# Two root-mean-square norms of a two-block transformer kernel: who sums the last tiles of squares, and when the first weight units are split

## What is computed

```python
def rmsnorm(x, g):
    y = x * rsqrt(mean(x * x, axis=-1) + EPS)
    return y * g

def first_block(x, ...):
    for i in range(2):
        h = rmsnorm(x, ln1_g[i]) @ w_in[i]          # cq, ckv, then the heads' k, q, v
        ...three groups of attention...
        x = x + concat(o_fox, o_diff, o_mla) @ w_o[i]
        up = causal_dwconv(rmsnorm(x, ln2_g[i]) @ w_up[i], ...)
        x = x + (silu(g) * u) @ w_down[i]
    return rmsnorm(x, final_g)

def second_block(x, c, ctx, ...):                   # ctx has 256 tokens
    for layer in range(2):
        h_lat = rms_norm(x, norm_g[layer]) * (1 + scale) + shift
        h_ctx = the same for ctx
        ...layer 0: mLSTM mixer; layer 1: windowed attention...
        x = x + gate * y
```

## Time and profile before

| | |
|---|---|
| median of 3 runs | 2538.12 us |
| the profiled execution | 2534.49 us |
| its span | 2532.8 us |
| mean granted clock of TensorE over the span | 0.993 |

### The profile page before, as it was taken

How to read it: one execution, slowest core, us unless ns; L and a number is a source line. 1 busy time by engine, 2 the same in 40 slices (tenths; PEclk the granted TensorE clock), 3 DMA queues, 4 the chain that set the end, 5 groups by cost and what they waited for, 6 DMA issues and landing times.

```text
span 2532.8 us, 32353 instructions
## 1 busy us (share of the span) xinstructions
PE 2466.3 (97%) x12450; PEld 2009.7 (79%) x12450; DVE 1217.8 (48%) x2205; ACT 986.0 (39%) x1731; POOL 977.3 (39%) x512
## 2 busy tenths in 40 slices
PE   9999999999999999999999999999999999899998
PEld 6986788888789678888888777878787778887766
DVE  4366599530245648974026522631251352556663
ACT  5465444432255545444333223131222322455552
POOL 3232365765433235576653223222222224322231
PEclk9999999999999999999999999999999999999999
DMA  4211254323321124532331111112111111111000
GB/s 177 67 55 67 92 189 169 101 94 98 116 67 55 67 84 150 192 111 96 105 119 57 52 42 59 51 34 67 51 59 42 50 50 46 58 59 34 30 21 34
DMA packets 54584, 200.48 MB, mean 79 GB/s; under 512 B 6176, under 2 KB 6176, under 8 KB 53664
## 3 DMA queue, kind: packets, MB, share of 16 engines
q1 hardware_dynamic: 52272, 189.27, 21.9%
q10 hardware_dynamic: 2160, 9.15, 1.0%
HBM read 196.29 MB, written 2.10 MB: 78 GB/s over the span
## 4 chain that ended last, share of the span: by engine, by line
PE 78%; DVE 15%; ACT 3%; issue 2%; POOL 2%; DVEq 0%; ACTq 0%; POOLq 0%
PE ps L890 25%; PE ps L557 19%; PE ps L577 16%; PE ps L607 11%; DVE arena L1953 7%; PE ps L782 2%; DVE arena L2142 1%; DVE arena L2139 1%; DVE norm_sq L1917 1%; PE ps L1203 1%; PE ps L798 1%; POOL norm_acc L2606 1%; POOL wl L2593 1%; DVE hl L1929 1%; PE ps L1007 1%
## 5 line engine op out<-in xcount | busy, mean ns | idle before, releaser
L2593 POOL TENSOR_TENSOR wl<-wring,wh 128x1024 fp32r<-128x1024 f32 (+1 forms) x305 | 770.0, 2525 | 1246.5 <-ACT wh L1243 1234.7
L1243 ACT ACTIVATE wh<-wring 128x1024 fp32r<-128x1024 f32 (+1 forms) x305 | 317.1, 1043 | 544.4 <-PE ps L890 307.9
L557 PE MATMUL ps<-hh,wh 128*128 128x512 f32 x768 | 300.6, 391 | 10.0 <-DVE hl L1929 5.1
L557 PE MATMUL ps<-hl,wh 128*128 128x512 f32 x768 | 299.8, 390 | 0.0
L557 PE MATMUL ps<-hh,wl 128*128 128x512 f32 x768 | 299.7, 390 | 0.0
L607 PE MATMUL ps<-arena 128*128 128x512 f32 (+2 forms) x912 | 264.8, 427 | 10.8 <-DVE arena L2115 4.8
L607 PEld LDWEIGHTS ps<-arena 128*128 128x128 f32 x912 | 141.8, 191 | 94.3 <-issue 76.1
L577 PE MATMUL ps<-hh,wh 128*128 128x512 f32 (+1 forms) x472 | 199.3, 422 | 5.0 <-DVE hl L2574 2.4
L1953 DVE CUSTOM_DVE_ANT_0 arena<-arena 128x1024 f32<-128x1024 f32 x96 | 182.6, 1902 | 8.6 <-DVE arena L2142 0.3
L577 PE MATMUL ps<-hh,wl 128*128 128x512 f32 (+1 forms) x472 | 186.6, 395 | 0.0
L577 PE MATMUL ps<-hl,wh 128*128 128x512 f32 (+1 forms) x472 | 185.9, 394 | 0.0
(11 more groups left out here) (342 smaller groups left out, 5219.4 us busy)
## 6 DMA issues: line engine op xcount, KB each, us to landing
wring<-wts SPq DMA_DIRECT2D x290, 512.0 KB, 3.3
arena<-wts SPq DMA_DIRECT2D x48, 512.0 KB, 4.0
wring<-wts SPq DMA_DIRECT2D x16, 384.0 KB, 2.9
xL<-xt SPq DMA_DIRECT2D x4, 512.0 KB, 5.3
arena<-tab SPq DMA_DIRECT2D x1, 2048.0 KB, 15.7
arena<-cv ACTq DMA_DIRECT2D x2, 1024.0 KB, 5.1
arena<-tab ACTq DMA_DIRECT2D x1, 2048.0 KB, 7.8
out_t<-xL ACTq DMA_DIRECT2D x8, 256.0 KB, 2.0
```

Source lines behind the costliest of these rows:

```text
L557: mm = nc.tensor.matmul(o[0], a, b, start=start and k == first and j == 0, stop=stop and k == last and j == 2)
L1243: nc.scalar.activation(wh[:, sn % SPLIT_SLOTS, :kn * w], raw(u)[:, :kn * w], ACT.Copy).then_inc(act_done, tick("act", ("hi", u)))
L2593: G.tensor_tensor(wl[:, sn % SPLIT_SLOTS, :kn * w], raw(u)[:, :kn * w], wh[:, sn % SPLIT_SLOTS, :kn * w].bitcast(F32), ALU.subtract).then_inc(
```

## The change

TensorE now sums the squares of the last tile (ln1 of layer 1, mL of layer 1) or the last two (ln2 of both layers): POOL adds up to the tile before, TensorE multiplies norm_acc by ones, and then the squares of the remaining tiles straight from norm_sq, into the same bank. On POOL the second lo of up 0 comes behind the remaining adds. On ScalarE hi(cq second) and hi(ckv first) of layer 0, hi(ckv first) of layer 1 and hi(akv 0 first) come ahead of the root, and hi(akv 0 second) ahead of the root of mC. mC takes its own bank (6) and is summed ahead of mL. The stirring ahead of the norms is shortened (10 to 4) or dropped (21 and 20), that behind mL is lengthened (6 to 13).

```diff
@@ -462,7 +462,12 @@
         tiles_of = {t: norms[t][1] for t in order}
 
         def norm_bank(tag):
-            return 6 if tag[0] == "fin" else 7
+            return 6 if tag[0] == "fin" or tag == ("mC", 1) else 7
+
+        late = {t: 0 for t in order}
+        late.update({("ln1", l): 1 for l in range(1, DEPTH)})
+        late.update({("ln2", l): 2 for l in range(DEPTH)})
+        late[("mL", 1)] = 1
 
         def split_norm(tag):
             return tag[0] in ("ln1", "ln2", "mC", "mL")
@@ -628,19 +633,25 @@
             def norm(tag):
 
                 nt, w = norms[tag][1:3]
-                if nt > 1:
-                    pe.wait_ge(pool_done, at("pool", "acc", tag, nt - 1))
+                n = nt - late[tag]
+                sq, acc, _ = scratch(tag)
+                if n > 1:
+                    pe.wait_ge(pool_done, at("pool", "acc", tag, n - 1))
                 else:
                     pe.wait_ge(act_done, at("act", "sq", tag, 0))
                 b = norm_bank(tag)
                 claim([b], "act", "ln", tag)
-                chain(ps[:, b, :w], [(ones[:], scratch(tag)[1][:, :w])], ("norm", tag))
+                last = nc.tensor.matmul(ps[:, b, :w], ones[:], acc[:, :w], start=True, stop=n == nt)
+                for m in range(n, nt):
+                    pe.wait_ge(act_done, at("act", "sq", tag, m))
+                    last = nc.tensor.matmul(ps[:, b, :w], ones[:], sq[:, m % 2, :w], start=False, stop=m == nt - 1)
+                last.then_inc(pe_done, tick("pe", ("norm", tag)))
 
             pe.wait_ge(pool_done, at("pool", "ones"))
 
             for l in range(DEPTH):
                 if l:
-                    stir(7, 10)
+                    stir(7, 4)
                     norm(("ln1", l))
                     stir(6, 13)
                 else:
@@ -822,7 +833,6 @@
                 pe.wait_ge(dve_done, at("dve", "ot", l, 7, 1))
                 for m in range(KT):
                     out_part(2, m, (2 + m) % 8)
-                stir(7, 21)
                 norm(("ln2", l))
                 stir(6, 13)
 
@@ -1070,10 +1080,9 @@
             for j, half in MO_ORDER[1][3:]:
                 mixed_out(1, j, half)
 
-            stir(0, 20)
+            norm(("mC", 1))
             norm(("mL", 1))
-            norm(("mC", 1))
-            stir(1, 6)
+            stir(1, 13)
 
             def ha_ready(k):
                 pe.wait_ge(dve_done, at("dve", "hl", ("mL", 1), k))
@@ -1301,17 +1310,18 @@
                         act.wait_ge(x_loaded[m // 2], 16)
                         nc.scalar.activation(x_sq[:, m, :], xL[:, m, :], ACT.Square).then_inc(
                             act_done, tick("act", ("sq", ("ln1", l), m)))
-                    split(("cq", l), slice(0, 1))
+                    split(("cq", l))
+                    split(("ckv", l), slice(0, 1))
                     act.wait_ge(prm_loaded, 16)
+                else:
+                    split(("ckv", l), slice(0, 1))
                 root(("ln1", l))
                 if l:
 
                     act.dma_start(arena[:, 0:TAB1], tab1).then_inc(tab1_loaded, 16)
                     high(("ln1", l), hH)
                 else:
-                    high(("ln1", l), hH, tiles=range(0, 2))
-                    split(("cq", l), slice(1, 2))
-                    high(("ln1", l), hH, tiles=range(2, KT))
+                    high(("ln1", l), hH)
                     nc.scalar.activation(fgn[:, 0:8], col("fin", 0, 8), ACT.Square).then_inc(act_done, tick("act"))
                     act.wait_ge(act_done, now("act"))
                     nc.scalar.activation(fgn[:, 0:8], fgn[:, 0:8], ACT.Ln, bias=col("eps")).then_inc(
@@ -1323,7 +1333,7 @@
 
                 act.wait_ge(dve_done, at("dve", "lamdot", l))
                 nc.scalar.activation(lamc[:, 2:4], lamc[:, 0:2], ACT.Exp).then_inc(act_done, tick("act", ("lamexp", l)))
-                split(("ckv", l))
+                split(("ckv", l), slice(1, 2))
                 square(("cq", l), 0, ("cn", l))
                 square(("cq", l), 1, ("cn", l))
                 split(("k", l, 0))
@@ -1703,13 +1713,12 @@
             square_mixed(4, 5)
             split(("aq", 0), second)
             square_mixed(6, 7)
+            split(("akv", 0), slice(0, 1))
             root(("mL", 1))
             high(("mL", 1), hH, 0)
+            split(("akv", 0), slice(1, 2))
             root(("mC", 1))
-            split(("akv", 0), slice(0, 1))
-            high(("mC", 1), hcH, 1, range(0, 4))
-            split(("akv", 0), slice(1, 2))
-            high(("mC", 1), hcH, 1, range(4, KT))
+            high(("mC", 1), hcH, 1)
             act.wait_ge(dve_done, at("dve", *last_scaled(("mC", 1))))
             act.dma_start(cut(ATT, TAB3), tab3).then_inc(tab3_loaded, 16)
 
@@ -2662,9 +2671,8 @@
                 split(("wo", l, 2, 0))
                 split(("wo", l, 2, 1))
                 split(("up", l, 0), slice(0, 1))
-                accumulate(("ln2", l), 1, 2, 3)
+                accumulate(("ln2", l), *range(1, KT - late[("ln2", l)]))
                 split(("up", l, 0), slice(1, 2))
-                accumulate(("ln2", l), 4, 5, 6, 7)
                 def gated_low(m):
                     pool.wait_ge(act_done, at("act", "guh", l, m))
                     pool.wait_ge(pool_done, now("pool"))
@@ -2687,7 +2695,7 @@
                         if last and (j, c) == (0, 0):
                             accumulate(("mC", 0))
                     if not last:
-                        accumulate(("ln1", l + 1), 2 * j, 2 * j + 1)
+                        accumulate(("ln1", l + 1), *range(2 * j, min(2 * j + 2, KT - late[("ln1", l + 1)])))
                     elif j < 3:
                         for m in (2 * j, 2 * j + 1):
                             accumulate(("mL", 0), m)
@@ -2746,7 +2754,8 @@
 
                 for m in tiles:
                     accumulate(("mC", 1), m)
-                    accumulate(("mL", 1), m)
+                    if m < KT - late[("mL", 1)]:
+                        accumulate(("mL", 1), m)
 
             split(("mo", 1, 1, 1))
             split(("mo", 1, 2, 0))
```

## The result

The changed kernel takes 2518.94 us (median of 4 runs, 2514.07 to 2522.34) against 2537.98 of the kernel before on the same chip: a ratio of 0.9922, 95% interval 0.9907 to 0.9936, 19.0 us less. The forecast was 2517.6 in a range of 2510 to 2526, faster. The runs of the changed kernel lie up to 8 us apart, those of before (40, timed beside the experiments) up to 12. The profiled execution of the changed kernel took 2522.3 us at a mean clock of 0.990, that of before 2534.5 at 0.993. By that figure the spans alone hide some 5 us of the gain (an estimate, 3 x 1.7), and what follows compares stretches between fixed points.

The account below looks back on a forecast made before the run. TensorE was taken as busy 97% of the span, so only some 66 us of idle, plus stirring, could be won. 2.1 - 1.0 + 4.0 + 6.8 + 8.6 = 20.5 us gave a median of 2517.6, range 2510 to 2526.

Parts of the forecast that it names:

- A: The start, first norm of layer 0: ckv's product starts 2.1 us earlier, less 1.0 for one low-clock stretch.
- B: ln1 of layer 1: gain 4.0 us, 2.6 from ckv starting earlier and 1.4 from a low-clock stretch that goes.
- The rule of two engines: Where POOL works in SBUF just ahead of VectorE's chain: VectorE starts at the lo's end less 0.2 us.
- C: ln2 in both layers: VectorE begins 3.4 us earlier in each, where POOL bounds now; 6.8 us in all.
- D: mL and mC: gain 8.6 us; akv's second unit 7.2 earlier, low clock 2.2, less 0.8 waiting for ScalarE.
- Costed at nothing: No separate term: extra TensorE pairs already in the sums, shortened stirring, lo of k and q, SyncE's loads.
- The clock rival: Half clock once behind each chain with stirring cut or moved (B, C twice, D), stays in A: 2525; chance 0.15.

Follow-up runs that it names:

- stir_only: The kernel before with only the stirring ahead of the norms cut (10 to 4, none at ln2 or mL): 2538.3 us, ratio 0.9987.
- ln2_only: The kernel before with only ln2's part (TensorE sums two tiles, lo of up 0 second behind the adds, no stirring): 2532.5 us, ratio 0.9969.
- splits_only: The kernel before with only ScalarE's order of the hi changed (cq second, ckv first, akv 0 both, ahead of the roots): 2525.1 us, ratio 0.9941.
- sums_back: The changed kernel with POOL adding the last tile again at ln1 of layer 1 and at mL: 2519.3 us, ratio 0.9913.
- after_again: The changed kernel once more, without an edit: 2517.9 us, ratio 0.9914.

## Why the prediction was right

- **The sum.** 20.5 us were forecast; the parts of the first profile give 0.9 + 4.6 + 3.3 + 3.1 + 9.0 = 20.8, those of the second 22.4. The medians give 19.0 and, on another chip, 20.6. The mechanism held in the main at all places. That the parts of the first profile meet the sum within 0.3 is in part luck: a low stretch of 1.5 that the changed kernel happened to have at A offsets one of 1.6 that the kernel before happened to have at B.
- **The rule of two engines** (VectorE starts at the lo's end less 0.2): the first scaling at A ended 0.57 us behind the last lo, so it ran from 18.3; 18.25 was said. At B it took 0.89, at C 1.23, at D the two took 1.99: delays of 0.14, 0.48 and 0.58 where 0.3, 0.3 and 0.65 were said. By the figure of the Trainium skill (SBUF — State Buffer, "A bandwidth-pool intuition that's wrong (but worth ruling out)"), which was measured with VectorE in front, each would have been 0.3 more, an estimate. The trace agrees with the blocking that the Trainium skill states (SBUF — State Buffer, "SBUF: two separate sides") and not with the longer wait.
- **A, 2.1 less 1.0:** 0.9 with a low stretch, 2.6 without. The net of 1.1 lies between them. Put on the load and the sum's end that the prediction used (hi of ckv at 14.1, TensorE's end at 14.8), the profiles without the stretch give 2.4 for the 2.1. The clock part is a chance and no term: the stretch cost 1.5 and came in two of the four profiles with this order and this gap. The root was to move by 0.25; in the first profile hi of ckv held it 0.9 behind TensorE's end.
- **B, 4.0:** 4.6. Counted from the last add of x by VectorE (663.00 and 663.11), the ones end 0.9 us earlier (666.89 against 666.10) and ckv starts 2.9 us earlier, where 2.6 were said. The low stretch was worth 1.6, as stir_only and ln2_only showed, where I had put 1.4. But it is a chance as well: of three profiles with the same wait of 2 us it fell in one, and it was that of the kernel before on which the sum was built. Without it B is 3.0.
- **C, 6.8:** 6.3 and 6.3 again. I had the time from the last add of x to the scaling 3.4 us shorter; it is 3.6 to 3.7, and the longer scaling gives 0.5 back.
- **D, 8.6:** 9.0. The first scaling's result is 2.1 us nearer, akv's second unit 7.7 instead of 7.2. The wait for the bank of the context tile is 0.35, not 0.8; in exchange the wait for the low part behind akv 0 grew by 0.5, which I had left out. The low stretch that went was put at 2.2 us and was of varying length: where it was 3.4 us instead of 6.8, in ln2_only, D was 0.76 shorter.
- **"Costed at nothing", the stirring:** wrong as a statement of its own. Cutting it costs 0.8 to 1.0 us at ln2 when the adds stay with POOL. It held only together with C's shorter sum, and I should have tied it to that.
- **The clock rival** (2525, chance 0.15) did not come: at B, C and D no profile of a kernel with the shortened sum at that place has a low stretch between the sum and the end of the part. Other low stretches moved: the first profile of the changed kernel has one of 6.8 us in the attention of layer 0 that the kernel before has not, and one execution differs from the next in them. This is not settled further: what puts them there was not tried.

## What to carry to other kernels

When several engines share in a sum that ends in one root, look at what stands in the queues behind the last addend: at ln2 two tiles left to TensorE, together with a weight's low part moved behind the adds, saved 3.2 us a layer; at ln1 and mL, where no low part was moved with it, one tile saved 0.8. Work that is pulled ahead of a wait is free only if all that it sets off is done, or shut out, before the chain behind the wait starts; here each lo that ran over the root's end came back as a longer first scaling, 0.1 to 1.8 us. And stirring has to be judged with the gap that it fills, not by itself.

## What was not expected

Stretches at half clock come and go from one execution to the next at the same place: at 21.3 us in one of two profiles of the changed kernel (a gap of 3.53 us ends at 20.60), and at 20.3 in splits_only, at the end of one of 2.42, while sums_back with 2.39 and after_again with 2.43 have none. At B it is the same: one of three profiles with a wait of 2 us has a low stretch behind it. They explain a good part of the spread of the runs: the lowest and the highest run of the changed kernel, 2514.07 and 2522.34, have mean granted clocks of 0.994 and 0.990. The kernel before had 0.993 at 2534.5 and 0.986 at 2545.9. A median of three that spans 0.6 us, as the one shown at the top, says little of this: the 40 runs timed beside the experiments gave 2533.8 to 2546.0, median 2539.5.
